# MLP output tiles computed two at a time, in turn into two of four PSUM banks

## The reference, cut to what matters

```python
def sq_relu_mlp(h, w1, w2):
    return jnp.square(jax.nn.relu(h @ w1)) @ w2

def reference(x, ...):
    for l in range(DEPTH):                       # DEPTH = 2
        h = rmsnorm(x, norm_gains[l, 0])
        m = hgrn2_gla_mixer(h, ...) if l % 2 == 0 else mla_mixer(h, ...)
        x = x + rmsnorm(m, norm_gains[l, 1])
        h = rmsnorm(x, norm_gains[l, 2])
        x = x + rmsnorm(sq_relu_mlp(h, mlp_w1[l], mlp_w2[l]), norm_gains[l, 3])
    return x
```

## Time and profile before

| | us |
|---|---|
| median of 3 runs (lowest, highest) | 1253.67 (1250.55, 1256.56) |
| the profiled execution, its own time | 1254.26 |
| its span, first to last instruction | 1252.5 |
| PE busy in the span | 1206.7 (96%) |
| DVE busy | 663.4 (53%) |
| ACT busy | 532.0 (42%) |
| mean granted TensorE clock, share of full speed | 0.990 |

### The profile page before, as it was taken

One profiled execution on the slowest core, in us unless ns is written; L12 is line 12 of the kernel. 1 busy time (PEld: TensorE's weight loads), 2 busy tenths in 40 slices (PEclk: granted clock), 3 DMA queues, 4 the chain that ended last, 5 costly groups with the idle time before them and its releaser, 6 DMA issues.

```text
span 1252.5 us, 16277 instructions
## 1 busy us (share of the span) xinstructions
PE 1206.7 (96%) x5995; PEld 995.9 (80%) x5995; DVE 663.4 (53%) x1028; ACT 532.0 (42%) x1049; POOL 114.3 (9%) x129
## 2 busy tenths in 40 slices
PE   6899999999999999999999998989999999999997
PEld 5677788887988888888888777767988888888886
DVE  4576867875663443443447257753653443443444
ACT  4554555454542332323436765543542332332332
POOL 2231212310380000000000000100000000000000
PEclk9999899999999999999999999999999999999999
DMA  4332121133333323323232122202323323333221
GB/s 122 102 84 56 47 67 52 51 119 126 101 101 102 94 96 96 100 100 87 98 101 77 54 79 61 68 18 68 101 101 101 99 92 96 100 100 89 95 85 68
DMA packets 87492, 108.23 MB, mean 86 GB/s; under 512 B 9186, under 2 KB 48195, under 8 KB 87428
## 3 DMA queue, kind: packets, MB, share of 16 engines
q1 hardware_dynamic: 85684, 101.85, 26.2%
q0 software_dynamic: 1744, 5.51, 1.4%
HBM read 104.20 MB, written 2.10 MB: 85 GB/s over the span
## 4 chain that ended last, share of the span: by engine, by line
PE 83%; DVE 7%; ACT 6%; issue 2%; DMA 1%; POOL 0%; DVEq 0%; SPq 0%; ACTq 0%
PE bank L1479 25%; PE bank L1481 25%; PE bank L1480 24%; PE pp L1621 1%; PE po L1899 1%; PE pp L1522 1%; PE pp L1479 1%; PE pp L1480 1%; PE pp L1481 1%; ACT w_hi L491 1%; ACT w_hi L489 1%; PE pp L1880 1%; DVE xl L1136 0%; DVE stat L1442 0%; PE po L1632 0%
## 5 line engine op out<-in xcount | busy, mean ns | idle before, releaser
L1479 PE MATMUL bank<-h_lo,w_hi 128*128 128x512 f32 (+4 forms) x572 | 218.5, 382 | 9.0 <-DVE h_lo L1079 4.4
L1480 PE MATMUL bank<-h_hi,w_lo 128*128 128x512 f32 (+4 forms) x572 | 215.3, 376 | 0.0
L1481 PE MATMUL bank<-h_hi,w_hi 128*128 128x512 f32 (+4 forms) x572 | 215.0, 376 | 0.0
L1479 PEld LDWEIGHTS bank<-h_lo,w_hi 128*128 128x128 f32 (+1 forms) x572 | 106.8, 187 | 31.4 <-issue 5.4
L1479 PE MATMUL bank<-wx,a_hi 128*128 128x512 f32 x320 | 126.3, 395 | 2.6 <-DVE wx L499 2.6
L1308 DVE TENSOR_TENSOR tmp<-sq,bank 128x512 f32<-128x512 f32 x64 | 44.0, 687 | 156.3 <-ACT sq L910 156.3
L1480 PE MATMUL bank<-wx,a_lo 128*128 128x512 f32 x320 | 125.2, 391 | 0.0
L910 ACT ACTIVATE sq<-bank 128x512 f32<-128x512 f32 x64 | 38.3, 598 | 204.6 <-PE bank L1481 204.6
L1481 PE MATMUL bank<-wx,a_hi 128*128 128x512 f32 x320 | 125.2, 391 | 0.0
L1481 PEld LDWEIGHTS bank<-h_hi,w_hi 128*128 128x128 f32 (+1 forms) x572 | 106.7, 187 | 19.9
L1479 PE MATMUL bank<-w_lo,a_hi 128*128 128x512 f32 x304 | 119.6, 394 | 2.5 <-DVE a_lo L1198 1.6
(11 more groups left out here) (312 smaller groups left out, 2059.3 us busy)
## 6 DMA issues: line engine op xcount, KB each, us to landing
stage<-in_mlp_w SPq DMA_DIRECT2D x128, 512.0 KB, 3.6
stage<-in_ev_w_in SPq DMA_DIRECT2D x28, 512.0 KB, 3.8
stage<-in_ev_w_out SPq DMA_DIRECT2D x8, 512.0 KB, 3.6
stage<-in_od_w_out SPq DMA_DIRECT2D x8, 512.0 KB, 3.5
stage<-in_od_w_in SPq DMA_DIRECT2D x10, 256.0 KB, 3.0
x_tok<-in_x SPq DMA_DIRECT2D x4, 512.0 KB, 4.8
xr<-in_x POOLq DMA_DIRECT2D x4, 512.0 KB, 3.8
gbc<-in_norm_gains POOLq DMA_DIRECT2D x4, 512.0 KB, 4.3
```

The lines of the kernel that those rows point to most:

```text
L1479: nc.tensor.matmul(dst, wh, xl_, start=first, stop=False)
L1480: nc.tensor.matmul(dst, wl, xh, start=False, stop=False)
L1481: return nc.tensor.matmul(dst, wh, xh, start=False, stop=last)
```

## The change

The MLP now uses four banks: the two of `bank`, `po` and `misc`; tile m goes to number m % 4 of them. PE computes tiles in pairs (m, m + 1). At each step k, the three products are issued for both tiles in turn, so that one matmul writes one bank and the next the other. PE waits before a pair until the tiles four places back have been read. Left single are tiles 0 and 1 of the first group, which are computed in parts while tokens are still arriving, and tiles 12 to 15 of the last group. What ACT and DVE do, and in which order, is the same, but for the names of the banks.

```diff
+        def mlp_banks(n0):
+            return [bank[n0 % 2], bank[(n0 + 1) % 2], po, misc]
...
-                            nc.scalar.activation(sq[:, m % 2, :], bank[n % 2][:, :], ACT.Relu).then_inc(relu_ready[layer], 1)
+                            nc.scalar.activation(sq[:, m % 2, :], m_bank[m % 4][:, :], ACT.Relu).then_inc(relu_ready[layer], 1)
...
+                def wait_m_bank(n, m, g, i):
+                    if g == 0 and m < 4:
+                        if m < 2:
+                            wait_bank(pe, n + m)
+                    elif i is None:
+                        wait_read(pe, n + m - 4)
+                    else:
+                        ready, value = read[n + m - 4]
+                        pe.wait_ge(ready, value + KD * (i - 1))
...
-                        ins = mm3(bank[n % 2][:, c], wh[:, k % 2, d], wl[:, k % 2, d], h_hi[:, k, c], h_lo[:, k, c],
-                                  k == 0, k == KD - 1)
+                        for w_, x_, first, last in ((wh, h_lo, k == 0, False), (wl, h_hi, False, False),
+                                                    (wh, h_hi, False, k == KD - 1)):
+                            for m in ms:
+                                d = slice(m % 4 * P, (m % 4 + 1) * P)
+                                ins = nc.tensor.matmul(m_bank[m % 4][:, c], w_[:, k % 2, d], x_[:, k, c], start=first,
+                                                       stop=last)
+                                if last and c.stop == T:
+                                    ins.then_inc(tile_done, 1)
...
+                    for m in range(2 if g == 0 else 0, KD, 2):
+                        wait_m_bank(n, m, g, i)
+                        wait_m_bank(n, m + 1, g, i)
+                        up(u, [m, m + 1], slice(0, T), m % 4 == 0, i)
+                    for q in range(0, KD, 2):
+                        if g == GROUPS - 1 and q >= NT:
+                            for one in (q, q + 1):
+                                wait_m_bank(n, KD + one, g, i)
+                                down(n, u, [one], g, i)
+                        else:
+                            wait_m_bank(n, KD + q, g, i)
+                            wait_m_bank(n, KD + q + 1, g, i)
+                            down(n, u, [q, q + 1], g, i)
```

More of the change, by code:

```diff
@@ L1307, in group @@
                                 dve.wait_ge(hid_ready[layer], m - 1 + KD * i)
-                            nc.vector.tensor_tensor(tmp[:, m % 2, :], sq[:, m % 2, :], bank[n % 2][:, :],
+                            nc.vector.tensor_tensor(tmp[:, m % 2, :], sq[:, m % 2, :], m_bank[m % 4][:, :],
                                                     ALU.mult).then_inc(hid_f32[layer], 1)
@@ L1312, in group @@
                             if first:
-                                nc.vector.tensor_copy(y[:, ys, :], bank[n % 2][:, :]).then_inc(y_ready[j], 1)
+                                nc.vector.tensor_copy(y[:, ys, :], m_bank[m % 4][:, :]).then_inc(y_ready[j], 1)
                             else:
                                 dve.wait_ge(y_ready[j], q + 1 + KD * (i - 1))
-                                nc.vector.tensor_tensor(y[:, ys, :], y[:, ys, :], bank[n % 2][:, :],
+                                nc.vector.tensor_tensor(y[:, ys, :], y[:, ys, :], m_bank[m % 4][:, :],
                                                         ALU.add).then_inc(y_ready[j], 1)
@@ L1732, in up @@
                         wh, wl = slot(v, T)
-                        d = slice(m % 4 * P, (m % 4 + 1) * P)
-                        if c.stop == T and c.start and m == 0:
+                        if c.stop == T and c.start and ms[0] == 0:
                             pe.wait_ge(x_split[j - 1], 7 + k // 4)
-                        elif c.start == 0 and c.stop < T and m == 0:
+                        elif c.start == 0 and c.stop < T and ms[0] == 0:
                             pe.wait_ge(x_split[j - 1], 5 + k // 4)
-                        ins = mm3(bank[n % 2][:, c], wh[:, k % 2, d], wl[:, k % 2, d], h_hi[:, k, c], h_lo[:, k, c],
-                                  k == 0, k == KD - 1)
@@ new lines, in down @@
+                def down(n, u, qs, g, i):
+                    h = qs[0] // NT
+                    lo_at = 0 if i is None else 16 * (i - 1)
+                    for k in range(KD):
+                        if qs[0] % NT == 0:
+                            pe.wait_ge(lo_ready, u + KD + 4 * h + k // 2 + 1 + lo_at)
+                        if qs[0] == 0:
+                            pe.wait_ge(hid_ready[layer], KD * (g if i is None else i) + k + 1)
+                        wh, wl = slot(u + KD + 4 * h + k // 2, T)
+                        for a_, w_, first, last in ((a_hi, wl, k == 0, False), (a_lo, wh, False, False),
+                                                    (a_hi, wh, False, k == KD - 1)):
+                            for q in qs:
+                                ins = nc.tensor.matmul(m_bank[q % 4][:, :], a_[:, k, tokens(q % NT)], w_[:, k % 2, :],
+                                                       start=first, stop=last)
+                                if last:
+                                    ins.then_inc(tile_done, 1)
+                        if k == TURN_AT and g == GROUPS - 1 and h == 1 and qs[0] % NT and layer == 0:
+                            turn_tokens(j, qs[0] % NT - 1)
@@ L1750, in group @@
                         for m in range(2):
[L1751 to L1770, removed]
+                            up(u, [m], slice(3 * P, T), False, i)
+                    for m in range(2 if g == 0 else 0, KD, 2):
+                        wait_m_bank(n, m, g, i)
+                        wait_m_bank(n, m + 1, g, i)
[9 more added lines that the diff above has]
+                            down(n, u, [q, q + 1], g, i)
                 group(0)
```

11 lines of the change are left out of this document (6 added, 5 removed).

## The result

The changed kernel takes 1256.3 us (median of 12 runs, 1254.3 to 1262.6), the kernel before 1252.1 (12 runs beside it, 1248.5 to 1256.6). The ratio is 1.0037, 95% interval 1.0023 to 1.0050: by that ratio 4.6 us slower (4.2 between the medians), inside what the prediction called "the same" (0.5%) but resolved by the runs. The forecast was 5.7 slower, 1259.4 from the 1253.67 known then; its rival "wait without the slow clock" said 4.1, 1257.8.

A forecast was written before the change was run, and what follows sets the result against it. PE was taken to bound the kernel. The terms 0 + 0 + 3.9 + 1.6 + 0.1 = 5.6, plus 0.1 for a first transpose's weight load, gave 5.7 us: 1253.67 + 5.7 = 1259.4 us. Range 1253 to 1263.5, the forecast's own 1257 to 1262.

The forecast's parts named there:

- the same: Whole kernel: a result within about 0.5% (6.3 us), not told from no change; chance 0.57.
- wait without the slow clock: Rival, end of layer 0's MLP: PE's wait comes but the clock holds; +4.1, 1257.8 us; chance 0.12.
- What bounds the kernel: Whole kernel: PE, busy 1206.7 us; the MLPs get shorter only if one matmul costs less.
- Term 1: Paired matmuls in both MLPs: alternating banks leaves starts 0.227 us apart; 0 us taken.
- The end of -37 us: Paired matmuls, other end of the bank term: 2784 matmuls each save 13.3 ns if repeated bank switches help.
- banks pay: Rival, paired matmuls: alternation gives back 13.3 ns each, the end's wait stays; 1222 us; chance 0.08.
- Term 2: MLP tile pairs: ACT and DVE get two tiles' evictions at once, but no wait comes; 0 us.
- Term 3: Layer 0's last group: late adds on DVE make PE wait at the transposes of t = 0; 3.9 us.
- The clock, 1.6: Behind PE's wait at layer 0's transposes: a stretch at 1.2 GHz, 1.6 us lost; ends 0 and 3.2.
- The prediction's own witness: Trace before: after 2.61 us idle, PE ran 694.98 to 698.39 at clock 0.50; 1.6 us lost.
- Term 4: Tile 12 in the last groups: weight unit 15 is barely ready; 0.1 us taken, left only in layer 1.

The follow-up runs named there:

- e3: The change with every tile single in the old order, the four banks still in rotation; ratio 1.0010 (0.9997-1.0022) to the kernel before.
- e1: The change with down tiles 8 to 11 of layer 0's last group single again; ratio 1.0023 (1.0009-1.0037) to the kernel before.
- e2: The change with all tiles single but one pair, tiles 10 and 11 of layer 0's last group; ratio 1.0040 (1.0026-1.0054) to the kernel before.
- e5: The change with tiles 6 to 15 of the last group single in both layers; ratio 1.0006 (0.9994-1.0017) to the kernel before.
- e6: The change with only 8 and 9 of the last group's down tiles still paired; 1255.2 us, one run.
- e7: The change with the next stage's first weight unit split behind tile 12 instead of tile 11; 1261.1 us, one run.
- e11: The change with 24 more wait-only instructions at the start of PE's program; ratio 1.0042 (1.0028-1.0056) to the kernel before.
- e8: The change with the next stage's first unit split behind tile 12 and the transposes two steps later; ratio 1.0019 (1.0006-1.0031) to the kernel before.
- e10: The kernel before with 24 more wait-only instructions at the start of PE's program; ratio 1.0005 (0.9988-1.0021) to the kernel before.
- e12: The kernel before, unchanged, run once more for a second profile; 1252.8 us, one run.
- e4: The change with layer 0's last-group transposes behind step k = 7 instead of k = 5; ratio 1.0029 (1.0011-1.0046) to the kernel before.

## Why the prediction was right, step by step

**What bounds the kernel** was right: PE is busy 1206.0 us, as before, and all that was lost are waits of PE.

**Term 1, banks, 0.** Right at the end taken: 0.22 or 0.23 us between starts within the pairs, PE busy 320.00 of 320 us, and e3. The end of -37 us, and with it the rival that banks pay, is gone. The Trainium skill's "TensorE: Matmul & The Clock Gate" warns in "A second HAM failure mode: psum-queue depth-cycling" of a clock that oscillates when banks are cycled, and puts it down to PE idling briefly between groups of matmuls. This case shows neither: the clock is 1.00 over 320 us in which nearly every matmul changes bank, and PE doesn't idle at the changes.

**Term 2, double evictions, 0.** Right for pairs behind pairs: no wait in the first MLP but the one of term 3. It holds through the pairing of the consumer, which the prediction used (42 matmuls to hidden tile 7) without saying that it is a condition; e1 pays 1.1 us of gap where that is missing.

**Term 3, the last group of layer 0.** The mechanism is the forecast one, and e2 and e5 show it from both sides. Point by point: the adds of tiles 10, 11 and 12 are 4.54 and 5.02 us apart (forecast 4.65 and 5.13; 5.44 and 5.44 in the earlier trace rows). PE is 0.86 us earlier up to there in this profile, so the add of tile 12 is late by 664.02 + 0.86 - 660.99 = 3.9 us (forecast 4.1). PE's wait is the gap of 3.12 less a matmul's 0.23, 2.9 us, not 3.9. The step that failed is that PE is at the transposes at 664.87, "0.3 us after they could go": I took the end of the *second* `new_x`, 664.57, but of PE's eight transposes for t = 0 the first four read only the half that the first `new_x` writes. That one ends at 663.16 + 0.75 = 663.91, and the slack was 664.87 - 663.91 = 0.96 us. With it the wait would have come out at 4.1 - 1.0 = 3.1. Some 0.3 is added because the second half is now awaited too, so that the matmul behind the transposes starts 1.07 us after them instead of 0.80. The same step is most of the difference in e6 (forecast 2.2, found 1.2). In e7 it points the same way (1.0 at the second transposes, found 0.7), but the size isn't worked out. With term 4's 0.1 the first MLP is 3.3 us longer in all.

**The clock, 1.6.** Right in size, wrong in being certain. Of the three profiles with this same wait, e2 and e11 have 3.41 us at clock 0.50 behind it and first MLPs 1.6 us longer (344.83 and 344.81 against 343.23), the change's own has not. So its worth is 0 or 1.6 in an execution; the rival "wait without the slow clock" and the forecast are both true, each at times. The prediction's own witness is no surer: the wait of 2.6 us behind the first MLP stands in all 14 profiles, and 1.2 GHz follows it in ten. In four (the change, e8, e10 and e12, which is the kernel before again) it doesn't. How often the clock falls in the change the timed runs can't tell: one such stretch is 0.0014 of the mean clock, and that is 0.987 to 0.995 from run to run.

**Term 4, unit 15.** In layer 0 0.1 was found, at tile 12. The prediction took 0.1 for what would be left in layer 1; there it is 0.4:

```profile
1228.81 1.23 DVE L502 TENSOR_TENSOR wx<-stage,wx 128x1024 fp32r<-128x1024 f32 x1 [2.41 <-ACT wx L492]
1229.59 1.00 PE L1774 MATMUL bank<-wx,a_hi 128*128 128x512 f32 x2
```

```profile
PEld bank L1774 <- DVE wx L502: 0.5, 1, 0.5
```

The first row is the low split of unit 15 behind tile 10, the second PE at the first of its matmuls; the line below is the wait of the weight load for it. The split starts 3.10 us after the add there (1225.71 to 1228.81) where I had carried over layer 0's 2.80; the 0.3 more arises between DVE's add and ACT's square behind it (1.08 us from start to start, 0.78 in layer 0), and why stays open. e5 and e6, where tiles 10 and 11 are single, don't have it.

**Not foreseen:** 0.8 us at the load of layer 1's output projection. The change edits nothing there; what it does alter is the length of PE's program, 5216 instructions instead of 5192, and by its waits the moments at which PE gets there.

**The sum** of the traces is 3.3 + 0.4 + 0.8 = 4.5 us, and 6.1 where the clock falls; measured 4.6, with an interval of 2.9 to 6.3 that holds both. (A load gap less 2.81 is its part.) The two profiles' spans, 1254.7 and 1252.5, differ by only 2.2 us, because the changed kernel's reaches the first MLP 0.9 us sooner and has the full clock behind the wait near 695, which saves it 1.4: neither comes from the change. For the others, by the same counting: e1 1.2 + 0.4 + 1.2 = 2.8, ratio 1.0022 (measured 1.0023); e2, clock loss included, 4.9, 1.0039 (measured 1.0040); e11, clock loss included, 4.9 + 0.4 - 0.1 = 5.2, 1.0042 (measured 1.0042); e4 1.8 (its 1.0 and the 0.8 behind the end) + 0.4 + 1.4 = 3.6, ratio 1.0029 (measured 1.0029); e5 the load's 1.3, 1.0010 (measured 1.0006); e8 0.4 + 1.5 = 1.9, 1.0015 (measured 1.0019). That the forecast of 5.7 was only 1.1 us off is thus partly luck: 1.0 too much wait and a clock loss of 1.6 that comes only at times stand against 0.3 at the second half, 0.3 more at unit 15 in layer 1 and 0.8 at the load, which it lacked.

No kernel whose ratio was measured is faster than the kernel before. e5, which has no wait of its own in the MLPs, is the same as it.

## What to carry to other kernels

Working two tiles at a time leaves PE's work as it is but hands the engines behind it two tiles at once, and later. That was free here wherever the consumer was paired too, and cost where a single step consumed it: look at the last group, where something reads tiles one by one, and there count to the exact instruction that releases the wait, not to the last one of its kind. Where matmuls already follow each other across bank switches in the same beat as within a bank, more banks brought nothing. And a difference of about 1 us in a stage that the change doesn't touch may come from where instruction fetches fall against a tightly timed load; it needn't belong to the idea of the change.

## What the runs showed of the hardware

- In seven of seven profiles in which a 16 KB fetch of PE's instructions begins within the flight of one 512 KB weight load with little slack, PE's gap there is 0.8 to 1.5 us longer; in the seven others, where the fetch begins before or after, it is not.
- 512-column matmuls start 226.7 ns apart whatever the bank, and 225.7 with two-byte views and weight loads of 96 instead of 188 ns. "TensorE: Matmul & The Clock Gate" of the Trainium skill, section "Back-to-back issue gap", has 215.8 by its formula, which it gives for a matmul by itself, and about 131 for a stream of weight loads and matmuls; the traces agree with neither.
- The same wait of 2.7 us was followed by 3.41 us at 1.2 GHz in two of three executions, at a cost of 1.6 us, and one of 2.6 us elsewhere in ten of fourteen.
